# Attention of one decoder layer: query block 1 in steps of four head pairs, block 0 in one step

## What is computed

```python
logits = einsum('bqngd,bqsnd->bqngs', qg, k_sel) * HEAD_DIM ** -0.5
logits = where(valid, logits, -inf)
p = softmax(logits, axis=-1)
o = einsum('bqngs,bqsnd->bqngd', p, v_sel)        # 8 heads of 64, 2 key/value heads
a = attend(q, k, v, qi, ki, wi)
mixed = sigmoid(ga) * (a @ w_pa) + sigmoid(gb) * (b @ w_pb)
x = x + mixed @ w_o
x = x + (silu(causal_dwconv(ua)) * ub) @ ffn_down
```

## Time and profile before

| | us |
|---|---|
| median of 3 runs | 1943.4 (1941.89 to 1946.81) |
| the profiled execution, its own time | 1954.15 |
| its span | 1951.9 |
| first score of the attention | 706.04 |
| first matmul of the projection by w_pa | 996.27 |
| PE busy | 1792.7 (92% of the span) |
| DVE, ACT, POOL busy | 1065.1, 510.8, 594.7 |

### The profile page before, as it was taken

How to read it: one execution, slowest core, us unless ns; L and a number is a source line. 1 busy time by engine, 2 the same in 40 slices (tenths; PEclk the granted TensorE clock), 3 DMA queues, 4 the chain that set the end, 5 groups by cost and what they waited for, 6 DMA issues and landing times.

```text
span 1951.9 us, 28410 instructions
## 1 busy us (share of the span) xinstructions
PE 1792.7 (92%) x11467; PEld 1683.2 (86%) x11467; DVE 1065.1 (55%) x1862; ACT 510.8 (26%) x744; POOL 594.7 (30%) x321
## 2 busy tenths in 40 slices
PE   4867899899999959888789999999999999999997
PEld 3734799899999847665579999999999999999997
DVE  3373675788888858766445344334344343344335
ACT  3252011121111245654433232111111111111115
POOL 0444133222213331132245115333333322323430
PEclk7888999999999979999989999999999999999998
DMA  7133211122222022253546111111111111111102
GB/s 250 39 93 90 50 48 39 44 72 90 85 77 56 15 98 88 87 174 122 170 146 223 44 33 55 55 43 43 43 43 43 48 49 32 54 43 38 38 16 89
DMA packets 130808, 144.59 MB, mean 74 GB/s; under 512 B 15981, under 2 KB 110925, under 8 KB 130309
## 3 DMA queue, kind: packets, MB, share of 16 engines
q1 hardware_dynamic: 113832, 77.56, 14.0%
q0 software_dynamic: 11920, 46.35, 7.1%
q10 hardware_dynamic: 4978, 19.59, 2.7%
HBM read 123.74 MB, written 19.13 MB: 73 GB/s over the span
## 4 chain that ended last, share of the span: by engine, by line
PE 58%; ACT 2%; DVE 1%; issue 1%; DMA 1%; another core or an unknown queue 0%; POOL 0%; DVEq 0%; ACTq 0%; SPq 0%
PE ps L229 47%; PE ps L1854 3%; PE ps L1898 2%; PE ps L1836 1%; PE ps L1820 1%; PE ps L1909 1%; PE ps L1935 1%; PE ps L1907 1%; DVE probs_turned L2120 0%; ACT probs L2042 0%; DMA gathered_kv<-in_cache_v,gather_rows 0%; ACT sample_probs L2004 0%; ACT sample_probs_turned L2014 0%; DVE probs L2191 0%
## 5 line engine op out<-in xcount | busy, mean ns | idle before, releaser
L229 PE MATMUL ps<-act_hi,w_hi 128*128 128x358 f32 (+1 forms) x1080 | 360.8, 334 | 13.9 <-POOL act_lo L461 8.4
L229 PE MATMUL ps<-act_lo,w_hi 128*128 128x358 f32 (+1 forms) x1080 | 354.7, 328 | 0.0
L229 PE MATMUL ps<-act_hi,w_lo 128*128 128x358 f32 (+1 forms) x1080 | 353.7, 327 | 0.0
L229 PE MATMUL ps<-x_gain_lo,w_hi 128*128 128x358 f32 x1056 | 344.8, 327 | 0.0
L229 PE MATMUL ps<-x_gain_hi,w_hi 128*128 128x358 f32 x1056 | 344.6, 326 | 0.0
L229 PE MATMUL ps<-x_gain_hi,w_lo 128*128 128x358 f32 x1056 | 344.4, 326 | 0.0
L545 POOL TENSOR_TENSOR w_lo<-w_raw,w_hi 128x1024 fp32r<-128x1024 f32 (+1 forms) x57 | 139.1, 2441 | 317.4 <-ACT w_hi L540 306.0
L229 PEld LDWEIGHTS ps<-act_hi,w_hi 128*128 128x128 f32 (+1 forms) x1080 | 204.4, 189 | 16.7 <-issue 11.6
L229 PEld LDWEIGHTS ps<-act_lo,w_hi 128*128 128x128 f32 (+1 forms) x1080 | 205.0, 190 | 1.2
L229 PEld LDWEIGHTS ps<-act_hi,w_lo 128*128 128x128 f32 (+1 forms) x1080 | 203.6, 189 | 0.9
L229 PEld LDWEIGHTS ps<-x_gain_lo,w_hi 128*128 128x128 f32 x1056 | 199.4, 189 | 0.2
(11 more groups left out here) (402 smaller groups left out, 3491.9 us busy)
## 6 DMA issues: line engine op xcount, KB each, us to landing
w_raw<-in_ffn_up SPq DMA_DIRECT2D x44, 512.0 KB, 3.9
w_raw<-in_w_in SPq DMA_DIRECT2D x32, 512.0 KB, 3.8
w_raw<-in_ffn_down SPq DMA_DIRECT2D x12, 512.0 KB, 3.4
w_odd_raw<-in_ffn_down SPq DMA_DIRECT2D x10, 512.0 KB, 3.5
x_save<-xt SPq DMA_DIRECT2D x1, 4296.0 KB, 12.9
mix_b<-row ACTq DMA_DIRECT2D x8, 537.0 KB, 3.7
sig_a<-row ACTq DMA_DIRECT2D x8, 537.0 KB, 3.0
sig_a_in<-sig_a ACTq DMA_DIRECT2D x8, 537.0 KB, 3.8
```

Source lines behind the costliest of these rows:

```text
L229: last = pe.matmul(core.acc(out_set)[0:rows, c, :], w(k), b(k)[:, c * CH:(c + 1) * CH], start=(k == 0 and n == 0), stop=(k == kblocks - 1 ...
```

## The change

The steps become a list. Step 0 and the 24 steps of blocks 7 to 2 stay; block 1 is done in two steps of two heads each, block 0 in one step of all four: 28 steps. A step's heads lie side by side in the score banks and in the probabilities, so that `pieces` of a short step are two, one for each key/value head, of four 128 x 128 tiles each. Masks and exponentials are still one instruction for each head and v. `evict` copies two heads in one instruction. The short buffers grow from 2048 to 4096 bytes and cover four weight tiles instead of two. The 98 sample items are dealt over steps 2 to 26 instead of 2 to 30. The split of the result starts at step 25, with columns 384 and on; block 2's columns follow at t = 28, and those of block 1 and block 0 at the very end. Block 1's inverses are spread in bank 1 at t = 28.

```diff
-    LASTQ, STEPS = NT - 1, 1 + G * (NT - 1)
+    LASTQ, SHORT = NT - 1, 2
+    steps = [(LASTQ, (0,))] + [(qb, (g,)) for qb in range(LASTQ - 1, SHORT - 1, -1) for g in range(G)]
+    steps += [(1, (0, 1)), (1, (2, 3)), (0, tuple(range(G)))]
+    STEPS, LONG = len(steps), 1 + G * (LASTQ - SHORT)
...
-    short_buffers = turned_buffers("short_turned", Map.C - 8192, 2048, SHORT, 128)
+    short_buffers = turned_buffers("short_turned", Map.C - 16384, 4096, G, 128)
...
-        if qb < 2:
-            return [((0, 1), range(qb + 1), 128)]
+        if qb < SHORT:
+            return [((v,), range(G), 128) for v in range(NKV)]
...
-    FIRST_ITEM, LAST_ITEM = 2, 31
+    FIRST_ITEM, LAST_ITEM = 2, STEPS - 1
...
-    SPLIT = STEPS - 4
-    EARLY, NEXT, OWN = slice(128 * SHORT, TP), slice(128, 128 * SHORT), slice(TP, TW)
+    SPLIT = STEPS - G + 1
+    EARLY, NEXT, OWN = slice(128 * (SHORT + 1), TP), slice(128 * SHORT, 128 * (SHORT + 1)), slice(TP, TW)
+    SECOND = slice(128, 128 * SHORT)
...
+            for m, g in enumerate(heads):
+                for a, width in chunks(NK[qb]):
+                    at = NK[qb] * m + a
...
+            for m in range(len(steps[s][1])):
+                out = core.flat(values_bank(m) , 512)[:, NKV * n * (m % 2):NKV * n * (m % 2 + 1)]
+                for k in tiles:
...
+            if t == STEPS:
+                spread_inverses(NT - SHORT, 1)
...
                 if g == 0:
-                    act.wait_ge(normed, NT - SHORT)
-                else:
-                    ahead.hi(act, g - 1)
+                    act.wait_ge(normed, NT - SHORT - 1)
+                    act.wait_ge(s_valued, 2 * (NGRP + 1) - 3)
+                elif g > 1:
+                    ahead.hi(act, g - 2)
...
             if t == STEPS:
-                act.wait_ge(normed, NT - 1)
+                ahead.hi(act, 2)
+                act.wait_ge(normed, NT - SHORT)
...
+        act.wait_ge(normed, NT - 1)
+        act.activation(core.rh[:, :, SECOND], raw[:, :, SECOND], ACT.Copy).then_inc(split_hi, 1)
         act.wait_ge(normed, NT)
         act.activation(core.rh[:, :, 0:128], raw[:, :, 0:128], ACT.Copy).then_inc(split_hi, 1)
...
+        pool.wait_ge(valued, STEPS - 1)
         ahead.lo(pool, 0)
-        pool.wait_ge(valued, STEPS)
-        pool.wait_ge(split_lo, G + 2)
+        pool.wait_ge(split_lo, G + 3)
```

More of the change, by code:

```diff
@@ L1729, in block_of @@
     def block_of(s):
-        return LASTQ if s == 0 else LASTQ - 1 - (s - 1) // G
+        return steps[s][0]
     def rows_of(s):
@@ L1736, in end_of, with width_of, stats, values_bank @@
     def end_of(b):
-        return G * b
+        return max(x for x, (qb, _) in enumerate(steps) if qb == LASTQ - b)
+    def width_of(s):
+        return NK[steps[s][0]] * len(steps[s][1])
+    def stats(s):
+        qb, heads = steps[s]
+        return [(m, slice(NK[qb] * m, NK[qb] * m + NK[qb]), 2 * (before[s] + m)) for m in range(len(heads))]
+    def values_bank(m):
+        return (5, 3)[m // 2]
     def first_bank(s, v):
@@ L1768, in block_ended @@
     def block_ended(t, lag):
-        return (t - lag) // G if 0 <= t - lag < STEPS and (t - lag) % G == 0 else -1
+        ends = [end_of(b) for b in range(NT)]
+        return ends.index(t - lag) if t - lag in ends else -1
     def columns(b):
@@ L1774, in columns @@
         return slice(128 * qb, 128 * qb + QROWS[qb])
-    weight = [3.6 - 0.15 * block_of(t) for t in range(STEPS)]
-    FIRST_ITEM, LAST_ITEM = 2, 31
+    weight = [3.6 - 0.15 * qb for qb, _ in steps]
+    FIRST_ITEM, LAST_ITEM = 2, STEPS - 1
     weight = [w if FIRST_ITEM <= t < LAST_ITEM else 0 for t, w in enumerate(weight)]
@@ L1815, in turn @@
             n, a = rows_of(s), 0
-            pe.wait_ge(exped, 2 * s + heads[-1] + 1)
+            pe.wait_ge(exped, 2 * before[s + 1] - NKV + heads[-1] + 1)
             after(pe, t_copied, count[s] + x)
@@ L1825, in score @@
         def score(s):
-            qb = block_of(s)
+            qb, heads = steps[s]
             n, q = rows_of(s), slice(128 * qb, 128 * qb + QROWS[qb])
-            after(pe, masked, 2 * s)
+            after(pe, masked, 2 * before[s])
             if s == 0:
                 pe.wait_ge(packed, 2)
[L1831 to L1837, removed]
+            for m, g in enumerate(heads):
+                for a, width in chunks(NK[qb]):
+                    at = NK[qb] * m + a
+                    for x, (half, ks) in enumerate(((0, hd.kqh), (0, hd.kql), (1, hd.kqh))):
+                        for v in range(NKV):
+                            p = slice(64 * v, 64 * v + 64)
+                            mine = last_q[half][p, :, :].rearrange("p g q -> p (g q)") if s == 0 else \
+                                (hd.kqh, hd.kql)[half][1 + g][p, q]
+                            last = pe.matmul(core.flat(first_bank(s, v), width_of(s), n)[:, at:at + width], mine,
+                                             ks[0][p, a:a + width], start=(x == 0), stop=(x == 2))
             last.then_inc(logits, 1)
```

94 lines of the change are left out of this document (51 added, 43 removed).

## The result

The changed kernel takes 1948.22 us (median of 10 executions, 1944.52 to 1952.11), the kernel before, on the same chip, 1943.16 us (10 executions, 1940.10 to 1946.81). The ratio is 1.0025, with a 95% interval of 1.0016 to 1.0034: slower by 5 us, about 0.25%. That lies within the 0.3% that the prediction called no change, and inside its range, but it is a loss where -0.2 us was forecast.

A forecast was written before the change was run, and what follows sets the result against it. PE limits the body, but the attention's end is bound by chains of engines waiting on each other. The sample chain 8.2 us shorter, the last 8.0 longer: -0.2 us, 1943.4 to 1943.2; range 1936.0 to 1950.5.

The forecast's parts named there:

- no change: Whole kernel: time within 0.3%, 5.8 us, of before; the forecast itself, with a chance of 0.57.
- mark 5: From v4 to R, the last sample item done: 16.8 us for 15.6, leaving R 8.2 us ahead of before.
- mark 1: End of the sample's key items: 9.5 us earlier, 937.15 becomes 927.7.
- Marks 1 and 2: Sample keys done 9.5 us earlier; first transpose of sample probabilities, t0, 9.1 us behind them as before, wait as long or longer.
- Marks 3 and 4: From t0 to the issue of the gather behind v1, 8.0 us for 6.8; from issue to v4, 11.2 for 12.3.
- Mark 6: From R's end to the first projection matmul: 23.3 us for 15.3, giving the gain back.
- The two `low` with POOL: Block 0's `low` in the last step, overlapped by POOL's weight split: 0.7 us added on the path.
- The slower one: Rival: dense items make key transposes wait for ACT's copies, +4.2 us; with gather and POOL lock 1949.2 us; chance 0.19.
- the faster one: Rival: thinner key waits, PE at 2.4 GHz, gather at its lower bound, -8.8 us together: 1934.4 us; chance 0.24.
- PE stays at 2.4 GHz: Part of the faster rival, from v4 to R on: 24 values and two spreadings quicker, -3.0 us.

The follow-up runs named there:

- the second trace of before: The kernel before, unedited, run and profiled again: median 1942.72 us, ratio 0.9995 to before; its profiled execution took 1945.76 us.
- the second trace of the changed kernel: The changed kernel, unedited, run and profiled again: median 1946.99 us, ratio 1.0016 to before.
- the second comparison: Both kernels run once more without edits: changed 1946.99 us, before 1942.72 us; ratio of changed to before 1.0016 [1.0007, 1.0024].
- the copies first: Changed kernel, from step 23 on ACT takes second-place sample copies ahead of the step's exponentials instead of behind: 1948.68 us, ratio 1.0030 to before.
- the deal alone: Kernel before with its 33 steps, only the sample items dealt over steps 2 to 26, nothing merged: 1949.02 us, ratio 1.0026 to before.

## Why the prediction was off

*Where the sum failed.* The terms should have added up to -0.2 us. Against the second trace of before they add up to +2.1 (+1.8 in the second trace of the changed kernel). The step that failed is mark 5, the wait and work from v4 to the end of R. It stood at +1.2 us in the sum (16.8 for 15.6) and measured +4.4 (18.0 for 13.7); the other terms together were 0.9 to 1.2 us better than forecast.

*The base.* The forecast read before's marks from one execution, and carried the difference over to the median. The prediction said how far the execution stood above the median, but took it for granted that all of the distance lay outside the terms. The second trace has 286.45 us of attention for 290.2. The keys' part of this, 2.5 us, does no harm, since mark 1 was worked out as a difference, and the changed kernel has it too (218.6 and 219.0 for 221.6). Of mark 5's error 2.0 us come from here: before's own 15.63 held the DMA wait of v6, 1.79 us, which the second trace does not have.

*Marks 1 and 2* hold: the keys 9.6 to 10.1 us earlier against the second trace for 9.5 forecast, t0 9.0 behind them, the wait longer (5.07 for 3.34) as said. The exponentials of 1032 columns are four, as in the earlier trace rows, and not five (the fifth item, e4, has no work on ACT), and e0 stands in step 21; as the 9.1 us were taken over whole, this changes nothing.

*Marks 3 and 4.* Each term is off by 1 to 2 us and their sum is not: 19.6 and 18.9 us for 19.2. That is luck: the path from t0 to the issue was longer, 9.6 us for 8.0 (from t0 to the end of the score 5.7 us, nearly all at the low clock, for 4.15), and the gather shorter, 10.0 and 9.4 us for 11.2. The wait of v4, forecast at about 3, was 2.76 and 2.16.

*Mark 5* in the changed kernel was mis-sized as well: from v4 to the end of R 18.04 us for 16.8. v4 and v6 of step 25 ended at 9.9 instead of 9.4 behind v4's start, and step 26 took 8.1 for 7.4; among the waits for ACT are the 1.14, 0.69 and 1.37 us in the rows of PE above. These 1.2 us and the 2.0 of the base are the error of the term. R is 6.0 to 6.3 earlier, not 8.2.

*Mark 6* came out as worked: 23.33 and 23.32 us for 23.3, and on the way too. Counted from R's end the spreadings start at 8.7 and 16.3 (9.0 and 16.2 in the sum), with 1.2 GHz in both sets of values, and exponentials at 0.39. The two `low` with POOL cost 0.76 us more (2.23 for 1.47) for 0.7.

*What the sum left out.* The traces give 1.8 to 2.1 us, the medians 4.3 and 5.1. The rest is not in a row of these traces, and the intervals leave it between 0 and 3 us in the second comparison and between 1 and 5 in the first. What the runs show is that the whole difference goes when the clock is held: 0.4 us between the kernels with the waits filled, for 3 to 5 without. One profiled execution, that with the copies first, had the last chain at 26.0 us with the instructions behind R unchanged. That the tail of the plain kernel falls as deep in executions that were not profiled would explain the rest; it was not seen in either of its own two traces, and stays open.

*The rivals.* The slower one named a loss, and its time of 1949.2 was near, but not its mechanism: the deal alone leaves the keys where the forecast had them. Of the faster one, "PE stays at 2.4 GHz", put at -3.0 us, was nearly the right price (20.7 for 23.3) of a clock that the kernel does not get by itself.

## What to carry to other kernels

Where a chain of small steps ends a stage, merging them trades overlap for fewer hand-overs. Here four heads in one step left PE waiting 2.5 to 3.6 us three times, with 24 matmuls between the waits, 21 of them at half the clock; two heads a step kept the overlap. Before working out a difference of two large terms, take a second execution of the kernel before: its two traces differ by 3.8 us in the very stretch that the change touches. And where PE waits for microseconds in a chain that it must go on with, filling the waits with work that nobody reads can be worth more than a new order of the work: 5 us here in the old order and 8 to 10 in the new, and both end at the same time. The filling must be shorter than the wait at the clock that it really gets: ten transposes took 2.33 us in a wait of 1.33.

## What the runs showed of the hardware

- The price of a low clock depends on what stands between the waits: filling the tail's waits gave 2.6 us in the chain with 24 matmuls of values between them (23.3 to 20.7), and 0 and 0.7 us in the one with single heads (15.26 to 15.22 and 14.53), where the clock went from 0.60 to 0.78 and 0.88 and the first filling ran past its wait.
- A raised clock is handed on: the matmuls of the projection behind filled waits took 0.33 us from the first on instead of 0.50, and what follows the attention was 1.5 to 1.6 us shorter in the two versions with only the tail's waits filled.
- Work alike does not get a clock alike: behind 2 us with 0.79 us of busy PE it was 0.50 in the trace with the copies first, and behind 2 us with 0.80 it stayed at 1.00 in that of the changed kernel.
- DVE and POOL held each other up for about whole instructions, in both directions: a pair of 1.59 us took 3.77, and POOL's 2.35 became 2.91.
